# Two fp32 transformer blocks on one Trainium2 core: the order of four VectorE products in the delta-rule stage, and two weight loads that trade places in the ring

## The reference

```python
# even mixer, gated delta rule (heads 6, chunk 64 in the reference)
decay = exp(where(incl, gam[..., :, None] - gam[..., None, :], -inf))
kk = einsum('bhnid,bhnjd->bhnij', kc, kc)
lower = eye(c) + where(strict, bc[..., :, None] * kk * decay, 0.0)
sol = triangular_solve(lower, rhs)
...
# odd mixer: diff attention (q_c, k_c, v_c) and gated linear attention (q_d, k_d, v_d, r_d)
q_c, k_c, v_c, q_d, k_d, v_d, r_d, g_d = split(x @ w_in, ODD_SPLITS)
...
# second block, for each of 4 half layers i
shift, scale, gate = split(silu(c) @ ada_w[i] + ada_b[i], 3)
```

## Time and profile before

| | |
|---|---|
| three runs | 1835.86, 1841.75, 1840.68 us (median 1840.68) |
| the profiled execution | 1835.86 us, span 1834.0 us from the first to the last instruction |
| PE busy | 1719.8 us, 94% of the span |
| DVE, ACT, POOL busy | 962.6, 655.4, 229.3 us |
| mean granted TensorE clock | 0.978 of full speed |
| DMA | 443.02 MB, mean 242 GB/s over the span |

### The profile page before, as it was taken

The page is one execution under the profiler, slowest core; times in us unless marked ns, Lnnn a source line. Parts: engine busy times, 40 slices in busy tenths (PEclk is TensorE's granted clock), DMA queues, the critical chain, the costliest instruction groups (busy, mean ns, idle before and its releaser), DMA issues. The chain is left out here.

```text
span 1834.0 us, 25552 instructions
## 1 busy us (share of the span) xinstructions
PE 1719.8 (94%) x10304; PEld 1275.5 (70%) x10304; DVE 962.6 (52%) x1789; ACT 655.4 (36%) x1102; POOL 229.3 (13%) x217
## 2 busy tenths in 40 slices
PE   7999999999999999999999979998799999899986
PEld 7788876799886655999888744443499897444433
DVE  1185643688541655887456553322367767433323
ACT  1036233467420335666356331111144464211101
POOL 0000000163120130453003102000001100100000
PEclk9999999999999999999999989999899999899998
DMA  7422286445434695355435649999834555799994
GB/s 294 159 93 92 93 306 245 184 175 217 161 142 157 230 384 211 140 207 185 160 115 223 236 193 419 420 420 420 331 116 161 184 207 209 315 419 420 420 420 180
DMA packets 51851, 443.02 MB, mean 242 GB/s; under 512 B 5900, under 2 KB 6160, under 8 KB 9104
## 3 DMA queue, kind: packets, MB, share of 16 engines
q1 hardware_dynamic: 47664, 426.79, 59.6%
q0 software_dynamic: 2480, 8.92, 1.4%
q10 hardware_dynamic: 1584, 5.61, 0.8%
HBM read 440.25 MB, written 1.05 MB: 241 GB/s over the span
## 5 line engine op out<-in xcount | busy, mean ns | idle before, releaser
L82 PE MATMUL ps<-ringx,arena 128*64 128x512 f32 x1056 | 277.0, 594 | 11.0 <-DMA ringx<-in_mu 3.8
L88 ACT ACTIVATE arena<-ps 128x384 f32<-128x384 f32 (+5 forms) x233 | 101.6, 436 | 490.7 <-PE ps L82 297.9
L82 PE MATMUL ps<-xsplit_f,wsplit_f 128*128 128x256 f32 x2112 | 258.6, 286 | 4.3 <-ACT xsplit_f L88 4.3
L82 PEld LDWEIGHTS ps<-xsplit_f,wsplit_f 128*128 128x128 f32 x2112 | 258.2, 195 | 4.8 <-ACT xsplit_f L88 4.8
L82 PE MATMUL ps<-ring,arena 128*64 128x512 f32 (+1 forms) x704 | 228.2, 597 | 7.9 <-DMA ring<-in_mu 7.7
L91 DVE TENSOR_TENSOR wsplit_f<-ring,wsplit_f 128x1024 fp32r<-128x1024 f32 x132 | 180.6, 1372 | 70.0 <-ACT wsplit_f L88 69.9
L82 PEld LDWEIGHTS ps<-ringx,arena 128*64 128x64 f32 x1056 | 88.9, 137 | 174.6 <-issue 154.4
L82 PE MATMUL ps<-xTs,ring 128*128 128x256 f32 (+1 forms) x960 | 187.4, 355 | 1.9 <-ACT xTs L88 1.8
L82 PEld LDWEIGHTS ps<-xTs,ring 128*128 128x128 f32 x960 | 162.8, 193 | 23.2 <-issue 5.8
L88 ACT ACTIVATE wsplit_f<-ring 128x1024 fp32r<-128x1024 f32 x132 | 138.2, 1051 | 57.5 <-PE ps L82 56.5
L91 DVE TENSOR_TENSOR ringlo<-ring,ringhi 128x1024 fp32r<-128x1024 f32 x88 | 120.5, 1385 | 58.4 <-ACT ringhi L88 58.1
(11 more groups left out here) (186 smaller groups left out, 2407.5 us busy)
## 6 DMA issues: line engine op xcount, KB each, us to landing
ring<-in_ada SPq DMA_DIRECT2D x24, 2048.0 KB, 8.4
ring<-in_wu SPq DMA_DIRECT2D x22, 2048.0 KB, 8.1
ringx<-in_mg SPq DMA_DIRECT2D x44, 1024.0 KB, 21.7
ringx<-in_mu SPq DMA_DIRECT2D x44, 1024.0 KB, 24.8
ringx<-in_md SPq DMA_DIRECT2D x44, 1024.0 KB, 26.1
ring<-in_md SPq DMA_DIRECT2D x24, 1024.0 KB, 25.5
ring<-in_mg SPq DMA_DIRECT2D x24, 1024.0 KB, 21.4
ring<-in_mu SPq DMA_DIRECT2D x24, 1024.0 KB, 23.9
```

Of the source, the lines that this page charges most:

```text
L82: return self.e.matmul(o, l, r, start=start, stop=stop, skip_group_check=True)
L88: return self.e.activation(o, i, f, **k)
```

## The change

It has two parts. In the loop of line 1776 DVE takes the units in the order 0, 1, 2, 3 instead of 1, 2, 3, 0. In `LOADS` W goes ahead of A2, and the two trade slots: W now has slot 2 and A2 has slot 0. So W now waits for A0's use, A2 for A1's, A4 (slot 2) for W's use and A5 (slot 0) for A2's. No other load changes its slot or its place, and PE's, ACT's and POOL's programs stay as they are.

```diff
@@ all_loads
-    out += [("wo", 0), ("wo", 1), ("wo", 2), ("wov", 0), ("wo", 3)] + ada[:3] + [("wov", 1)] + ada[3:]
+    out += [("wo", 0), ("wo", 1), ("wo", 2), ("wov", 0), ("wo", 3)] + ada[:2] + [("wov", 1)] + ada[2:]
...
-ELSEWHERE = {("ada", 2, 2): 2, ("wov", 1): 0}
+ELSEWHERE = {("wov", 1): 2, ("ada", 2, 2): 0}
...
@@ vector, even
                     if k == 0:
-
-                        for i in (1, 2, 3, 0):
+                        for i in range(4):
                             v.wait_ge(*a("gdDT", i))
                             v.wait_ge(*t("gdb", i))
                             tt(E.u[i]["LT"], E.u[i]["DT"], ps("gdb", i)[:, 0:384], ALU.mult).then_inc(s_dve, v.did("free", "gdb", i))
```

## The result

The changed kernel takes 1852.07 us (median of 7 runs, 1847.52 to 1856.28) against 1840.68 us (7 runs, 1835.86 to 1843.73). The ratio is 1.0066, with a 95% interval from 1.0047 to 1.0086, so the change costs about 12.1 us by the ratio, and 11.4 us by the two medians. 1850.8 us and 10.1 us were forecast. The profiled execution has a span of 1847.2 us, 13.2 more than before.

A forecast was written before the change was run, and what follows sets the result against it. PE, busy without gaps from 205 us, was taken to bound the delta rule, and the transfer rate the odd mixer's burst. 3.95 + 1.2 + 4.9 = 10.1 us on the median 1840.68 gave 1850.8 us, range 1844 to 1857.

The forecast's parts named there:

- The loop: Delta rule: `conv` 19 waits for the bank that DVE's product of unit 1 empties; PE stands still 3.95 us.
- The clock behind it: Delta rule, after PE's stall: TensorE's clock may fall to half speed, costing 1.2 us, bounds 0 and 3.4.
- W and A2: Odd mixer: W's earlier load gains 0, and A2's later load costs 0 with 13 us of margin.
- A4's wait: Odd mixer: A4 now waits for W's second half, lands at 652.1 and makes PE wait 2.7 us.
- The burst: Odd mixer: eight `ada` loads instead of seven at 426 GB/s; the last lands 4.9 us later, A4's wait included.
- the last lands one load later, and PE gets there in time: Odd mixer: A11 lands 4.9 us later; PE needs 30.2 us of its own from A4 and has 35.8.
- waits for these loads of 7 to 9 us in all: Odd mixer, sign to look for: PE's waits for `in_ada` total 7 to 9 us against 3.3 before.
- 5.6 us ahead in my account: Odd mixer, A4 to A11: PE's spare 5.6 us go into waits at A5, A7 and A11.
- 6.5 us as an upper bound: Odd mixer: the loads cost up to 6.5 us if a clock fall lands behind PE's last spare us.
- The premise that slots do not interrupt the burst: Odd mixer: the tightest slot, A11's, frees at A8's use; A8 lands at 673.2, its use takes 1.9 us.
- the figure of the Trainium skill that the prediction set aside: Odd mixer loads: about 358 GB/s would make the extra load 5.9 us; set aside for the windows' 426 GB/s.

The follow-up runs named there:

- loop_1_first: Kernel before with only DVE's loop changed, to the order 1, 0, 2, 3; ratio 0.9998 (0.9989 to 1.0007).
- loop_short: Kernel before with only the loop in order 0, 1, 2, 3, plus 4 unread matmuls in PE's stall before `conv` 19; ratio 1.0017 (1.0005 to 1.0030).
- a4_free: Kernel before with W early in slot 2 and A2 in slot 0, but A4 in slot 0 and A5 in slot 2; ratio 1.0019 (1.0005 to 1.0032).
- loads_filled: Kernel before with only W and A2 trading slots and places, plus 6 unread matmuls before A4's wait; ratio 1.0037 (1.0024 to 1.0050).
- a5_first: Kernel before with the change's loads only, but A5 ahead of A4 in SP's order and in A2's slot; ratio 1.0023 (1.0014 to 1.0033).
- before_filled: Kernel before plus 4 unread matmuls in front of A7's wait; ratio 1.0004 (0.9995 to 1.0014).
- loads_only: Kernel before with only W and A2 trading slots and places, the loop as before; ratio 1.0036 (1.0023 to 1.0049).

## Why the prediction was right, and which term was short

**The loop (3.95 us).** Right in mechanism and size: 3.84 us of idle at `conv` 19, ended by DVE's second product. loop_1_first shows that the bank is the cause and the delay of DVE is not: by itself that delay cost 0.3 us.

**The clock behind it (1.2 us).** Right in sign, a little short: 1.8 us in the trace, 1.7 by loop_short, and none of it was hidden by DVE.

**W and A2 (0 and 0).** W's wait did not exist before and does not after. From A0's first matmul to the end of W's last PE takes 44.5 us in both profiled executions (644.68 - 600.16 and 650.33 - 605.81), so in the trace the early load gains and costs nothing. The time of a4_free (1.0019) is not explained by this, and a small cost stays open.

**A4's wait (2.7 us).** 2.66 us.

**The burst (4.9 us).** This is the term that was mis-sized: 7.2 us in the trace. The step "the last lands one load later, and PE gets there in time" holds only while PE keeps its clock behind A4's wait (loads_filled, 43.2 us). The prediction had waits for these loads of 7 to 9 us in all; there are 2.7. In the changed kernel PE's matmuls from A4 to A5 take 10.3 us (3.64, 1.87, 1.63 and 3.13) and not 5.8, and those of A8 with the columns behind them 1.6 us more; the waits for DVE grow from 1.2 to 3.2 us; the load waits of 3.3 us go. That is 4.5 + 1.6 + 2.0 - 3.3 = 4.8 us, where the start of A11 less the start of A4 grew by 38.05 - 33.55 = 4.5, and A4's own wait comes on top. PE was 5.6 us ahead in my account, and two falls of the clock and the waits for DVE used more than that. I had kept 6.5 us as an upper bound for just this and then summed without it, and the measured 7.2 us is above even the bound. The premise that slots do not interrupt the burst failed too: A11 went at 687.0, when A8 was used, and the transfers fell to 254 GB/s. In its profiled execution a5_first takes the extra load away and gets nothing for it, which no theory of rate allows. All in all the mechanisms of both parts held. The sum was 3 us short of the 13.0 us in the trace, and the total came out in the range although the largest term was a third too small.

The Trainium skill (TensorE: Matmul & The Clock Gate, "HAM oscillation — how this bites in real kernels") describes this pattern: a wait for a transfer between groups of matmuls lets the clock gate close, and the next group starts cold. The trace agrees at A4, where 2.66 us of waiting are followed by windows at 0.61, 0.50 and 0.61, but not every wait for a load is followed by a fall: behind the 1.36 us at A11 the windows of the kernel before stay at 1.00.

By the figure of the Trainium skill that the prediction set aside (DMA: Bandwidth & Descriptors, "Where 436 GB/s comes from", about 358 GB/s for HBM to SBUF) a load more would be 5.9 us, an estimate. loads_filled measures 4.9 us, and its 4 us windows from 652 to 680 us show 418 to 442 GB/s.

## What to carry to other kernels

Where products take PSUM banks in rotation, the order in which the readers run decides which later product stalls: count a full turn ahead, and read first what the next product's bank holds. Before a load is moved behind another buffer's last use, ask whether it leaves idle transfer time for a full stretch, and price the wait with the clock that follows it, not by its length alone. In the loop a stall of 3.84 us cost 5.8 us, its length and half again. Unread matmuls gave back 1.7 us there when they fitted the stall and lost time when they were twice as long; where the transfers set the end they gave nothing, and as added work they are here a test more than a remedy.

## What the runs showed that I had not expected

The clock's falls move from one execution to another. The same loads gave 49.3 us from A0 to A4 in one execution and 54.9 us in another, with waits of PE for DVE of 0.6 to 1.1 us in both; only the second had low windows there (0.86 and 0.83 on average). The kernel before shows it by itself: before_filled has its loads and, up to A7, its matmuls, and took 51.8 us from A0 to A4 in its execution (0.86 from 600 to 612 us) against 49.3. The whole difference need not reach the end: in loads_only A0 came 2.7 us earlier than in the kernel before, so that of 5.6 us some 3 were left at A4. Such differences may be a part of the spread between executions of one kernel (7.9 us for the kernel before, in the seven runs above), but this was seen in single traces and not counted.
